# A three-stage transformer kernel: the last recurrent tile by token halves, and reordered starts and ends of four stages

## The chip, the cores and the metric

One core of a Trainium2 chip runs the whole program in one launch. The metric is the device time in microseconds (us). The engines are TensorE (PE), VectorE (DVE), ScalarE (ACT), GpSimd (POOL) and SyncE (SP, which issues all DMAs here). All data is float32.

## What is computed

A sequence of 1024 tokens with 1024 features passes two blocks of two layers each. Cut to what the change touches:

```python
def rglru_layer(x, norm_g, w_in, conv_w, conv_b, w_rg, b_rg, w_ig, b_ig, lam, w_out):
    h = rms_norm(x, norm_g)
    u = h @ w_in                                    # 1024 -> 2 * 1280
    xb, gate = u[..., :D_RNN], u[..., D_RNN:]
    xb = causal_depthwise_conv(xb, conv_w, conv_b)  # 4 taps
    r, i = sigmoid(blocks(xb) @ w_rg + b_rg), sigmoid(blocks(xb) @ w_ig + b_ig)
    log_a = -LRU_C * r * softplus(-lam)
    a, bterm = exp(log_a), sqrt(-expm1(2.0 * log_a)) * (i * xb)
    _, hs = lax.associative_scan(_lin_combine, (a, bterm), axis=1)
    return (hs * silu(gate)) @ w_out                # 1280 -> 1024, then x + ...
```

Then come a latent attention layer (its output projection is called `out_b` below), the final norm of the first block (`final1`), a layer of eight differential attention heads beside a chunked state space scan, a sliding window attention layer (its output projection is `out_sw`), and the last RMS norm (`final2`), whose result is stored.

## The kernel before

**Tiles.** Activations lie with features on partitions: 8 tiles of 128 features x 1024 tokens (`resid`). Each product runs at float32 accuracy as three passes: `w_hi*x_hi`, `w_hi*x_lo`, `w_lo*x_hi` (lines 197 to 199), each a 128x512 matmul. A 128-column weight tile (128x1024, `w_raw`) is loaded by DMA into one of two slots, split by ACT into `w_hi` (line 186) and by DVE into `w_lo` (line 192); one whole tile is 48 matmuls. Of the activations, ACT writes the high part (`operand_hi`) and DVE the low part (`operand_lo`). Every engine has its own program order, written out by hand; semaphores join them.

**Start.** `begin` reads the eight input tiles. For each, ACT writes `operand_hi` (line 319) and the square (line 326), DVE writes `operand_lo` (line 340) and adds the square to a sum (line 348), in turn. PE runs the first weight tile behind them into `acc[0]`, then the second into `acc[1]`; two of its eight slices in, it sums the squares over partitions (line 236), and after the fourth it spreads the norm's diagonal (line 244). ACT copies that to SBUF as `factor`.

**Recurrent layer.** `rglru` loops over b = 0..9, 128 channels each. PE: x tile b+1, the two gates' matmuls of b (line 1045, 3.6 us), gate tile b+1. DVE: `u = acc * factor` (line 1148), three taps, the split of the next weights, gate arithmetic, the scan over 1024 tokens (`tensor_tensor_scan`, line 1201) and `y` (line 1204). For b = 0 the first use of `acc[0]` waits for `factor`.

**Its tail.** The output projection `out_a` (`project_halves`) multiplies ten channel tiles by 16 weight tiles: q = 0..7 for the first 512 tokens, q = 8..15 for the second. It starts in b = 9: operands 0 to 8 are `y` of earlier b read back from HBM into `out_a_raw`; operand 9 is `rnn_y` itself. ACT and DVE split operands 0 to 5 (`Ahead.count`) inside `rglru`, 6 to 9 after it. PE runs q = 0 and 1 side by side for six slices, then the last four slices of each. q = 2 uses the slot of q = 0, and its split stands in both engines' order behind operands 10 and 11 (tokens 512 on), which SP loads after `y` of b = 9 has been stored.

**Head stage.** `out_b` ends with `final(1)`: DVE scales the second token half of `resid` by the first block's norm (line 866, eight instructions), and then all engines meet at a barrier. `differential_attention` starts with v and q tiles done, in `acc[0]` and `acc[1]`. PE's first work is the first half of the k tile (`key_half(0, 0)`) into `acc[0]`, so it waits until ACT has copied v out (line 2187). DVE then takes the low parts of q (line 2240), copies the positional rows into `da_kb` (line 2311) and `da_qb`, and takes the low part of the keys (line 2251); only then come the first scores (line 2018).

**End.** In `out_sw`, the last tile (q = 15) is followed by its residual add, its square, 8 small products with the sum of squares (lines 633 and 636), the newton steps (lines 365 to 369), the spread (line 644), eight scalings of 128x512 (line 844) and eight stores (line 605).

## Time and profile before

| what | value |
|---|---|
| runs of the kernel | 2520.18 us median of 3 (2518.3 to 2521.41) |
| the profiled execution: time / span | 2522.0 us / 2520.2 us |
| PE busy | 2418.8 us, 96% of the span |
| DVE, ACT, POOL busy | 1610.2, 1203.2, 181.8 us |
| mean granted TensorE clock | 0.985 of full speed |

A share of the span is a mean over stages; what counts for a change is where PE stands idle and what it waits for there. The granted clock of a stretch is 1.00 at 2.4 GHz and 0.50 at 1.2 GHz.

### The profile page before, as it was taken

To read this page: it belongs to the slowest core of one execution; us is meant where nothing else is said; L and a number is where in the kernel's file an instruction comes from. 1 tells how busy PE (TensorE), PEld (TensorE's weight loads), DVE (VectorE), ACT (ScalarE), POOL (GpSimd) and SP (SyncE) were. 2 spreads that over 40 slices of the span, in tenths; PEclk is the share of its full clock that TensorE was granted. 3 is DMA by queue.
4 is the path that set the end of the run, shared out by engine and by line. 5 is a ranking of instruction groups with operands and counts; after the bars stand their busy time and mean duration, and the time that the engine had idled before them with its cause. 6 is when DMAs were issued, how large, how long until landed. Compare 5 with 4: busy or idle time off the path is not lost. (4 is left out here: it accounts for less than half of the span.)

```text
span 2520.2 us, 31828 instructions
## 1 busy us (share of the span) xinstructions
PE 2418.8 (96%) x12061; PEld 2003.2 (79%) x12061; DVE 1610.2 (64%) x2946; ACT 1203.2 (48%) x2167; POOL 181.8 (7%) x109
## 2 busy tenths in 40 slices
PE   7999899998999999899999999999999999999998
PEld 5777687887888877688888888888787787888776
DVE  6766656436666657666666666653566665888874
ACT  4555533224544543456555555431554534565542
POOL 0000021000000052000000000000112130000022
PEclk9999999999999999899999999999999999999998
DMA  3222332112221331111101111224543421111133
GB/s 132 80 71 88 127 94 68 61 68 87 79 87 51 113 111 57 42 43 34 43 26 42 34 43 34 83 100 148 192 148 133 142 93 45 34 51 51 51 129 110
DMA packets 91891, 203.22 MB, mean 81 GB/s; under 512 B 10208, under 2 KB 43104, under 8 KB 90720
## 3 DMA queue, kind: packets, MB, share of 16 engines
q1 hardware_dynamic: 91744, 201.25, 23.5%
q8 instruction: 94, 1.54, 0.3%
q14 instruction: 53, 0.43, 0.1%
HBM read 160.26 MB, written 40.96 MB: 80 GB/s over the span
## 5 line engine op out<-in xcount | busy, mean ns | idle before, releaser
L197 PE MATMUL acc<-operand_hi,w_hi 128*128 128x512 f32 x1822 | 739.2, 406 | 42.1 <-DVE w_lo L192 12.7
L199 PE MATMUL acc<-operand_hi,w_lo 128*128 128x512 f32 x1822 | 716.4, 393 | 0.0
L198 PE MATMUL acc<-operand_lo,w_hi 128*128 128x512 f32 x1822 | 715.2, 393 | 0.0
L197 PEld LDWEIGHTS acc<-operand_hi,w_hi 128*128 128x128 f32 x1822 | 345.5, 190 | 120.2 <-issue 19.4
L199 PEld LDWEIGHTS acc<-operand_hi,w_lo 128*128 128x128 f32 x1822 | 344.6, 189 | 75.2
L198 PEld LDWEIGHTS acc<-operand_lo,w_hi 128*128 128x128 f32 x1822 | 345.6, 190 | 68.1 <-issue 3.6
L192 DVE TENSOR_TENSOR w_lo<-w_raw,w_hi 128x1024 fp32r<-128x1024 f32 (+2 forms) x205 | 231.6, 1130 | 173.6 <-ACT w_hi L186 171.8
L186 ACT ACTIVATE w_hi<-w_raw 128x1024 fp32r<-128x1024 f32 (+2 forms) x205 | 199.5, 973 | 275.0 <-PE aux L199 149.0
L197 PE MATMUL aux<-operand_hi,w_hi 128*128 128x512 f32 x634 | 257.4, 406 | 22.5 <-DVE w_lo L192 6.0
L199 PE MATMUL aux<-operand_hi,w_lo 128*128 128x512 f32 x634 | 249.5, 394 | 0.0
L198 PE MATMUL aux<-operand_lo,w_hi 128*128 128x512 f32 x634 | 249.2, 393 | 0.0
L197 PEld LDWEIGHTS aux<-operand_hi,w_hi 128*128 128x128 f32 x634 | 120.5, 190 | 54.5 <-DVE w_lo L192 13.2
L198 PEld LDWEIGHTS aux<-operand_lo,w_hi 128*128 128x128 f32 x634 | 120.7, 190 | 26.2 <-issue 2.4
L199 PEld LDWEIGHTS aux<-operand_hi,w_lo 128*128 128x128 f32 x634 | 120.3, 190 | 26.0
L2267 DVE TENSOR_REDUCE att<-aux 128x1 f32<-128x256 f32 (+7 forms) x128 | 96.3, 752 | 36.4 <-PE aux L2022 36.1
L2215 ACT ACTIVATE da_pth<-acc 128x512 f32<-128x512 f32 (+2 forms) x96 | 43.8, 490 | 128.6 <-PE acc L2036 128.2
L3286 ACT ACTIVATE sw_pth<-aux 128x512 fp32r<-128x512 f32 x64 | 38.3, 599 | 110.9 <-PE aux L3199 110.9
L884 DVE TENSOR_TENSOR resid<-aux,resid 128x512 f32<-128x512 f32 x55 | 37.9, 689 | 78.7 <-PE aux L199 78.5
L2547 DVE SCALAR_TENSOR_TENSOR ssd_work<-ssd_work,vec 128x1024 f32<-128x1024 f32 x36 | 46.3, 1285 | 45.3 <-ACT ssd_work L2526 42.2
L2046 PEld LDWEIGHTS acc<-da_v,da_pth 128*128 128x128 f32 x576 | 71.0, 196 | 3.7 <-ACT da_pth L2215 1.1
L1624 PE MATMUL acc<-mlah_pth,mlah_v 128*128 128x256 f32 (+1 forms) x320 | 70.1, 366 | 2.6 <-ACT mlah_pth L1747 1.6
L2046 PE MATMUL acc<-da_v,da_pth 128*128 128x128 f32 x576 | 71.4, 280 | 0.7 <-ACT da_pth L2215 0.7
(432 smaller groups left out, 4060.3 us busy)
## 6 DMA issues: line engine op xcount, KB each, us to landing
w_raw<-in_stream SPq DMA_DIRECT2D x201, 512.0 KB, 3.7
ssd_e<-cs_scratch SPq DMA_DIRECT2D x8, 1024.0 KB, 6.7
g_scratch<-ssd_work SPq DMA_DIRECT2D x12, 512.0 KB, 2.9
ssd_xbc<-g_scratch SPq DMA_DIRECT2D x8, 768.0 KB, 4.8
y_scratch<-rnn_y SPq DMA_DIRECT2D x10, 512.0 KB, 2.6
out_a_raw<-y_scratch SPq DMA_DIRECT2D x20, 256.0 KB, 4.2
resid<-in_x SPq DMA_DIRECT2D x8, 512.0 KB, 8.5
g_scratch<-mlai_g SPq DMA_DIRECT2D x8, 512.0 KB, 2.9
```

Source lines behind the costliest of these rows:

```text
L186: act.activation(k.w_hi_sb[:, t.slot, 0:width], k.w_raw[:, t.slot, 0:width], ACT.Copy).then_inc(k.w_hi[t.slot], 1)
L192: dve.tensor_tensor(k.w_lo_sb[:, t.slot, 0:width], k.w_raw[:, t.slot, 0:width], as_f32(k.w_hi_sb[:, t.slot, 0:width]), ALU.subtract).then_ ...
L197: pe.matmul(out, w_hi, x_hi, start=first, stop=False)
L198: pe.matmul(out, w_hi, x_lo, start=False, stop=False)
L199: return pe.matmul(out, w_lo, x_hi, start=False, stop=last)
L884: dve.tensor_tensor(resid(q), total(q), resid(q), ALU.add).then_inc(k.acc_free[t.slot], 1)
L1624: mm = pe.matmul(out_v[:, q], v[:, kt * P:(kt + 1) * P], pth[g_ % 2][:, kt, q], start=kt == 0, stop=kt == 2 * g_ + 1)
L2046: mm = pe.matmul(out_v[:, e * P:(e + 1) * P], pth[:, kt, e * P:(e + 1) * P], v[:, kt * P:(kt + 1) * P], start=kt == 0, stop=kt == 2 * g_ + e)
L2215: act.activation(pth[:, at:at + w, (t % 2) * P:(t % 2 + 1) * P], slots[at // 4][:, 0:w * P].rearrange("p (n q) -> p n q", q=P), ACT.Copy). ...
L2267: dve.reduce_max(st[:, 0, :], k.aux[:, m, 0:att_keys(t)], AX.X).then_inc(s["top"], 1)
L2547: link(dve.scalar_tensor_tensor(out=xc[:, :], in0=u[:, tap:tap + S], scalar=k.vec[:, bass.ds(VEC["conv_w2"] + 12 * tap + b, 1)], in1=xc[:, ...
L3286: act.activation(pth[:, n % 2, :], turned, ACT.Copy).then_inc(s["pth"], 1)
```

## The change

Five places, all of the same arithmetic:

1. `begin`: weight tile 0 is loaded first and split first; ACT and DVE split all eight input tiles before any square is taken; the sum of squares is read by PE after six slices of the second tile, the spread comes behind that tile. `acc[0]` is copied raw into `rnn_u`, and the norm's factor is applied there.
2. `rglru`, b = 9: the gates' Tanh move ahead of the silu's Tanh; the last of scaling, scan and `y` run by token halves, with operands 6 to 9 split in between; SP loads operands 10 to 15 in front of the last store of `y`. PE runs eight slices of q = 0 and 1 side by side instead of six.
3. `out_b`: `final(1)` goes. ACT keeps the factor (`kept_factor`), and each of the eight steps of head 0 does one of the eight scalings.
4. `differential_attention`: the first half of head 0's keys goes into the free bank `aux[1]`, second half; three slices of the second half stand before the scores; POOL copies the positional rows; DVE's q work is reordered.
5. `out_sw`: tile 15 runs by quarters of 256 tokens, each with its own sum, factor, scaling and stores.

`begin`: SP, PE and ACT.

```diff
+        sp.dma_start(k.w_raw[:, 0, :], k.stream[0]).then_inc(k.w_loaded[0], 16)
+        sp.dma_start(k.vec[:, :], vec).then_inc(s["vecs"], 16)
         for d in range(DT):
             sp.dma_start(k.resid[:, d, :], x_t[d]).then_inc(s[f"x{d}"], 16)
...
-            if kt == 1:
+            if kt == DT - 1:
+                mm.then_inc(k.tile_done[tiles[1].slot], 1)
+            if kt == 5:
                 pe.wait_ge(s["fill"], 6)
                 pe.wait_ge(s["sum"], DT - 1)
                 stats_pe_sum(pe, k, s, 0, ss, 0)
-            if kt == 3:
-                stats_pe_spread(pe, k, s, 0, rb)
-        mm.then_inc(k.tile_done[tiles[1].slot], 1)
+        stats_pe_spread(pe, k, s, 0, rb)
...
+        act.wait_ge(k.tile_done[tiles[0].slot], 1)
+        act.activation(ahead.u[:, 3:S + 3], k.acc[:, 0, :], ACT.Copy).then_inc(k.acc_free[tiles[0].slot], 1)
         stats_act(act, k, s, 0)
```

`rglru`: SP in front of the last store, and DVE in b = 9 behind its last full-width instruction.

```diff
+                for q in range(RNN_TILES, 16):
+                    ahead.load_y(sp, q)
             sp.wait_ge(s["y"], b + 1)
...
+        ahead.low(dve, 6)
+        dve.wait_ge(s["bi"], last + 1)
+        dve.wait_ge(s["root"], last + 1)
+        scaled_input(0)
+        dve.wait_ge(s["bt0"], 1)
+        dve.tensor_tensor_scan(thr[:, half(0)], a[:, half(0)], bi[:, half(0)], 0.0, ALU.mult, ALU.add
+                               ).then_inc(s["scan0"], 1)
+        ahead.low(dve, 7)
+        dve.wait_ge(s["scan0"], 1)
...
+        gated(0)
+        ahead.low(dve, 8)
+        ahead.low(dve, 9)
+        scaled_input(1)
+        dve.wait_ge(s["bt"], last + 1)
+        dve.tensor_tensor_scan(thr[:, half(1)], a[:, half(1)], bi[:, half(1)], thr[:, HALF - 1:HALF], ALU.mult, ALU.add
+                               ).then_inc(s["scan"], 1)
+        dve.wait_ge(s["scan"], last + 1)
+        gated(1)
```

`project_halves`: PE's lead in `out_a`, and ACT and DVE at the end of `out_b`.

```diff
-            for kt in range(0 if sequential else kts - 4):
+            rest = kts - (2 if done else 4)
+            for kt in range(0 if sequential else rest):
...
         roots(1)
+        if double:
+            act.wait_ge(s["rb"], 2)
+            act.activation(k.kept[:, :], factors(1, 0), ACT.Copy)
...
-        if double:
-            final(1)
```

`differential_attention`: PE, POOL, DVE's first work, and DVE's step t.

```diff
         key_half(0, 0, range(DT))
+        key_half(0, 1, range(3))
         pe.wait_ge(k.acc_free[q_tile(0).slot], q_tile(0).before + 1)
         turn_values(0)
         scores(0, 0)
-        key_half(0, 1, range(DT))
+        key_half(0, 1, range(3, DT))
...
+    @block.gpsimd
+    def _(pool):
+        pool.wait_ge(s["tab_k"], 16)
+        for m in range(2):
+            pool.tensor_copy(kb[64:128, m, :], g[64:128, :]).then_inc(s["kbr"], 1)
...
-        for n in range(2):
-            queries(0, n, k.acc[:, 1, :])
-        dve.wait_ge(s["tab_k"], 16)
-        for m in range(2):
-            dve.tensor_copy(kb[64:128, m, :], g[64:128, :]).then_inc(s["kbr"], 1)
         dve.wait_ge(s["tab_q"], 16)
         first = k.vec[64:128, VEC["slope8"]:VEC["slope8"] + 1]
         dve.tensor_scalar(qb[64:128, 0, :], o[64:128, 0, :], first, None, ALU.mult)
+        queries(0, 0, k.acc[:, 1, :])
         dve.tensor_scalar(qb[64:128, 1, :], o[64:128, 0, :], first, None, ALU.mult).then_inc(s["qbr"], 1)
+        queries(0, 1, k.acc[:, 1, :])
         keys(0, 0)
...
+                if not b:
+                    x = k.resid[:, t, half(1)]
+                    dve.scalar_tensor_tensor(out=x, in0=x, scalar=k.vec[:, VEC["final1"] + t:VEC["final1"] + t + 1],
+                                             in1=k.kept[:, :], op0=ALU.mult, op1=ALU.mult)
```

`project_halves` for `out_sw`: PE in tile 15, and DVE.

```diff
+            for c in range(2):
+                for kt in range(DT):
...
+                    if c and kt == 3:
+                        quarter_squares(0)
+            quarter_spread(0)
+            quarter_squares(1)
+            quarter_spread(1)
...
+            quarter_variance(0)
+            quarter_factor(0)
+            dve.wait_ge(k.tile_done[t.slot], t.before + 1)
+            dve.tensor_tensor(quarter(resid(final_q), 1), last_total[1], quarter(resid(final_q), 1), ALU.add
+                              ).then_inc(k.acc_free[t.slot], 1)
+            dve.wait_ge(s["rb"], 2)
+            for d in range(3):
+                quarter_scaled(0, d)
+            quarter_variance(1)
+            quarter_scaled(0, 3)
+            quarter_factor(1)
+            for d in range(4, DT):
+                quarter_scaled(0, d)
+            dve.wait_ge(s["rb"], 3)
+            for d in range(DT):
+                quarter_scaled(1, d)
```

How the instructions move at two places. First DVE in b = 9 of the recurrent layer, before (`rnn_thi` holds the scan's input, `out_a_lo` with `rnn_y` is operand 9, the last `w_lo` is q = 2's):

```order
L1189 SCALAR_TENSOR_TENSOR rnn_t<-rnn_a,rnn_t 128x1024
L1196 SCALAR_TENSOR_TENSOR rnn_thi<-rnn_thi,rnn_a 128x1024
L1201 SCALAR_TENSOR_TENSOR rnn_y<-rnn_a,rnn_thi 128x1024
L1204 SCALAR_TENSOR_TENSOR rnn_y<-rnn_y,rnn_sg 128x1024
L562 TENSOR_TENSOR operand_lo<-out_a_raw,operand_hi 128x512 x2
L562 TENSOR_TENSOR out_a_lo<-out_a_raw,out_a_hi 128x512
L562 TENSOR_TENSOR out_a_lo<-rnn_y,out_a_hi 128x512
L562 TENSOR_TENSOR operand_lo<-out_a_raw,operand_hi 128x512 x2
L192 TENSOR_TENSOR w_lo<-w_raw,w_hi 128x1024
```

and in the changed kernel:

```order
L573 TENSOR_TENSOR operand_lo<-out_a_raw,operand_hi 128x512
L1339 SCALAR_TENSOR_TENSOR rnn_thi<-rnn_thi,rnn_a 128x512
L1352 SCALAR_TENSOR_TENSOR rnn_thr<-rnn_a,rnn_thi 128x512
L573 TENSOR_TENSOR operand_lo<-out_a_raw,operand_hi 128x512
L1344 SCALAR_TENSOR_TENSOR rnn_y<-rnn_thr,rnn_sg 128x512
L573 TENSOR_TENSOR out_a_lo<-out_a_raw,out_a_hi 128x512
L573 TENSOR_TENSOR out_a_lo<-rnn_y,out_a_hi 128x512
L1339 SCALAR_TENSOR_TENSOR rnn_thi<-rnn_thi,rnn_a 128x512
L1363 SCALAR_TENSOR_TENSOR rnn_thr<-rnn_a,rnn_thr,rnn_thi 128x512
L1344 SCALAR_TENSOR_TENSOR rnn_y<-rnn_thr,rnn_sg 128x512
L573 TENSOR_TENSOR operand_lo<-out_a_raw,operand_hi 128x512 x2
L192 TENSOR_TENSOR w_lo<-w_raw,w_hi 128x1024
```

Operands 6, 7 and 8 no longer stand behind the whole scan, operand 9 needs only its first half, and the second half stands before q = 2's weights. Second, PE at the start of the heads, before (the first line is the last pass of the first half of the keys):

```order
L199 MATMUL acc<-operand_hi,w_lo 128x512
L1997 MATMUL acc<-ident,da_vt 128x128 x8
L2018 MATMUL aux<-da_ka,da_qa 128x128
L2020 MATMUL aux<-mask_r,ident_r 128x128
L2022 MATMUL aux<-da_kb,da_qb 128x128
```

and in the changed kernel:

```order
L199 MATMUL aux<-operand_hi,w_lo 128x512
L197 MATMUL acc<-operand_hi,w_hi 128x512
L198 MATMUL acc<-operand_lo,w_hi 128x512
L199 MATMUL acc<-operand_hi,w_lo 128x512
L2157 MATMUL acc<-ident,da_vt 128x128 x8
L2180 MATMUL aux<-da_ka,da_qa 128x128
L2182 MATMUL aux<-mask_r,ident_r 128x128
L2184 MATMUL aux<-da_kb,da_qb 128x128
```

The first half of the keys is now written to `aux`, and three slices (nine matmuls, of which three are shown) of the second half come ahead of the turning of v.

## Rows read from the trace of the kernel before

**Rows 1.** The page: PE's busy time, its share, its instructions.
```profile
PE 2418.8 (96%) x12061; PEld 2003.2 (79%) x12061; DVE 1610.2 (64%) x2946; ACT 1203.2 (48%) x2167; POOL 181.8 (7%) x109
```
**Rows 2.** Waits of PE over the span: total us, times, longest us.
```profile
PE acc L197 <- ACT da_vt L2187: 8.1, 1, 8.1
...
PE aux L197 <- DVE out_a_w2l L538: 4.2, 1, 4.2
...
PE aux L2018 <- DVE da_kb L2251: 2.5, 1, 2.5
```
**Rows 3.** Timeline, start and early recurrent layer: start us, us, instruction [idle before].
```profile
9.86 0.80 PE L197 MATMUL acc<-operand_hi,w_hi 128*128 128x512 f32 x1 [9.86 <-DVE w_lo L192]
...
23.56 0.50 PE L197 MATMUL acc<-operand_hi,w_hi 128*128 128x512 f32 x1 [0.67 <-DVE operand_lo L340]
...
28.17 0.50 PE L197 MATMUL acc<-operand_hi,w_hi 128*128 128x512 f32 x1 [0.62 <-DVE w_lo L192]
...
31.07 1.84 PE L236 MATMUL aux<-inv_col,stat_sq 128*128 128x1 f32 x16
...
54.17 1.22 DVE L192 TENSOR_TENSOR w_lo<-w_raw,w_hi 128x1024 fp32r<-128x1024 f32 x1
...
54.42 3.60 PE L1045 MATMUL aux<-rnn_xc,rnn_r 128*128 128x512 f32 x8
...
80.45 1.22 DVE L192 TENSOR_TENSOR w_lo<-w_raw,w_hi 128x1024 fp32r<-128x1024 f32 x1
```
**Rows 4.** Waits of DVE from 75 to 262 us, the recurrent layer.
```profile
DVE rnn_u L1148 <- PE acc L199: 28.9, 7, 4.4
```
**Rows 5.** Timeline of the recurrent layer's tail.
```profile
285.67 2.29 DVE L1201 TENSOR_TENSOR_SCAN rnn_y<-rnn_a,rnn_thi 128x1024 f32<-128x1024 f32 x1
...
289.88 0.79 PE L197 MATMUL acc<-operand_hi,w_hi 128*128 128x512 f32 x1 [4.97 <-DVE operand_lo L562]
...
299.70 1.23 DVE L192 TENSOR_TENSOR w_lo<-w_raw,w_hi 128x1024 fp32r<-128x1024 f32 x1 [0.33 <-ACT w_hi L186]
```
**Rows 6.** Windows: stretch, length, PE, PEld, DVE, ACT, POOL busy, clock, DMA share, GB/s.
```profile
301.40:306.90 5.50, 5.50 (x13) 4.34 (x14) 4.29 (x5) 3.55 (x6) 2.41 (x2) 0.50 0.36 119
...
1027.40:1033.90 6.50, 6.50 (x18) 5.35 (x19) 3.15 (x10) 3.35 (x8) 0.00 (x0) 0.50 0.26 83
...
2505.10:2512.20 7.10, 4.59 (x15) 2.93 (x14) 1.94 (x11) 0.20 (x1) 0.00 (x0) 0.50 0.00 0
```
**Rows 7.** Timeline of the start of the heads.
```profile
1008.79 5.35 DVE L866 SCALAR_TENSOR_TENSOR resid<-resid,vec,aux 128x512 f32<-128x512 f32 x8
...
1015.42 1.02 ACT L2187 ACTIVATE da_vt<-acc 128x1024 f32<-128x1024 f32 x1 [7.80 <-PEq L85]
...
1021.47 1.29 DVE L2311 CAST da_kb<-da_g 64x1024 fp32r<-64x1024 f32 x2
...
1026.53 0.69 DVE L2251 TENSOR_TENSOR da_kb<-acc,da_ka 64x512 fp32r<-64x512 f32 x1 [0.54 <-ACT da_ka L2137]
```
**Rows 8.** DMA issues from 1015 to 1020 us: KB, us to landing.
```profile
da_o<-in_tables SPq DMA_DIRECT2D x1, 256.0 KB, 4.1
```
**Rows 9.** POOL's groups by form: busy us, mean ns.
```profile
L782 POOL MEMSET stat_sq<- 128x1024 f32 x4 | 3.8, 958 | 811.9 <-PE acc L1624 411.5 <-DMA y_scratch<-stat_sq 347.5 <-PE aux L244 37.8
L1335 POOL TENSOR_TENSOR stat_sq<-stat_sq,mlai_sq 128x1024 f32<-128x1024 f32 x1 | 2.8, 2757 | 35.2 <-ACT mlai_sq L1372 35.2
```
**Rows 10.** Timeline of PE: 256-column passes, and the end.
```profile
2136.93 0.28 PE L197 MATMUL aux<-sw_pth,sw_v_hi 128*128 128x256 f32 x1
2137.05 0.28 PE L198 MATMUL aux<-sw_ptl,sw_v_hi 128*128 128x256 f32 x1
...
2502.35 0.39 PE L198 MATMUL aux<-operand_lo,w_hi 128*128 128x512 f32 x1
...
2502.58 0.39 PE L199 MATMUL aux<-operand_hi,w_lo 128*128 128x512 f32 x1
```
**Rows 11.** Timeline of DVE: the last scalings.
```profile
2512.14 5.36 DVE L844 SCALAR_TENSOR_TENSOR resid<-resid,vec,aux 128x512 f32<-128x512 f32 x8 [2.17 <-PE aux L644]
```

More of the change, by code:

```diff
@@ L448, in project_halves @@
     own = own or {}
+    end = after == "end"
+    final_q = tiles - 1
     if "raw" in own:
@@ L1165, in _ @@
                 dve.wait_ge(s["y"], b)
+            if b == last:
+                split_lo(dve, k, g_tile(b + 1))
+                for q in range(2):
+                    ahead.low(dve, q)
             dve.tensor_tensor(sg[:, :], k.acc[:, g.slot, :], factor[:, :], ALU.mult
@@ L3477, in build @@
         if stop > 2:
[L3478 removed]
+            heads_and_ssd(k, tables, kept)
         k.end_layer()
```

234 lines of the change are left out of this document (166 added, 68 removed).

## The prediction

> **What bounds the kernel.** I read PE's busy share first: 96% [rows 1], so the bound is PE, and only some 100 us of the span can be won without fewer matmuls. Then PE's waits [rows 2]: the reader should look for single long ones, since the change adds no matmul and takes none away. Three lie where the change works: 8.1 and 2.5 us at the start of the heads, 4.2 us in the recurrent tail. A long wait is followed by a stretch at half clock: 0.50 for 5.5 and 6.5 us [rows 6]. Last come the places themselves in order of time [rows 3, 5, 7, 10, 11], each read for what PE waits for there, and what would be late next. A pass of 512 columns takes 0.23 us at full clock [rows 10], so a slice of two banks (six passes) takes 1.37, a tile 10.9.
>
> **1. Start.** PE's first tile starts at 9.86, the second at 28.17 [rows 3]. Seven times it stands about 0.67 us for DVE [rows 3], which makes an `operand_lo` and a sum in turn, and each restart costs some 0.15 more; without them the tile takes 18.3 - 4.7 - 1.0 = 12.6. With the sums moved behind, DVE needs 1.2 to 1.3 per slice, less than PE. ACT's first split starts no later, since weights and table load come ahead of it. First matmul at 9.9, second tile at 22.5: 5.6 us ahead. But nothing behind it starts earlier by that much. Seven sums chained at 1.26 from about 22.0 end at 30.8, and PE reaches its sixth slice at 30.7; the squares' sum stood at 31.07 [rows 3]. So `factor` comes 0.2 us earlier, and all of DVE's work on b = 0 hangs on it. PE's first gates would be done at 52.6 instead of 54.42 + 3.60 = 58.0, and the gate tile's weights are low-split at 54.17 + 1.22 = 55.4 [rows 3]: 2.8 of the lead are gone. One b later PE arrives at 55.4 + 10.9 + 10.9 + 3.6 = 80.8, and the weights are ready at 80.45 + 1.22 = 81.7, where before PE came at 54.42 + 3.60 + 21.8 + 3.6 = 83.4. From then on DVE has slack, 4.4 us per b [rows 4], and the lead holds. **Gain 1.7 + 0.2 = 1.9, I take 1.8.**
>
> **2. Recurrent tail** (times of before). The root ends at 285.67 - 1.3 = 284.4 [rows 5] in both kernels: ACT's gates come earlier, but the root hangs on a chain that the silu's Tanh joins. Before, scaling 1.2, scan 2.3 and `y` 1.2 in full [rows 5], then operands 6 to 9; PE stood 4.97 us [rows 5], then ran 24 passes, the first at a slower pace, to 301.4 - 4.2 = 297.2 [rows 2, 6]. Now DVE does low 6 (0.6, done 285.6), half scaling 0.7, half scan 1.2, low 7 (288.0), half `y` 0.7, low 8, low 9 (290.0). PE takes slices 6 and 7 of both tiles at 285.6 and 288.0, then 12 passes: done at 292.1. The next tile needs DVE's second half (0.7 + 1.2 + 0.7), two lows 1.2, `w_lo` 1.2 and its piece 0.4: 290.0 + 5.4 = 295.4. Before, `w_lo` started at 299.70 [rows 5], because its ACT split stood behind operands loaded after the last store, and PE resumed at 301.4. **Gain 6.0.** PE still stands 3.3 us, so I keep the half clock of 5.5 us behind it [rows 6]; it costs 2.75, which is the bonus if it goes. SP now waits for seven lows in front of the store of `y`; that store comes at 292.6, nobody reads it before operand 19, and q = 4's weights behind it land before q = 2 ends.
>
> **3. Start of the heads.** PE ended at 1016.6 - 8.1 = 1008.5 [rows 2], DVE's eight scalings at 1014.1, and ACT began the stage at 1015.42 [rows 7], 1.3 after DVE. Without them DVE's last work ends at 1008.9, so the stage starts at 1010.2, and PE at once, having a bank of its own: 6.3 us sooner than at 1016.6. ACT's copy of the factor, 0.6, lies in its wait for the first scaling. Then the chain: tables land 4.1 us after issue [rows 8], at 1013.9; DVE's qb row 0.75, q half 1.4, row 0.75, q half 1.4: 1018.1; second key low part 0.7 + 0.7: scores at 1019.5. PE meanwhile does 24 + 9 passes (7.5) and 1.0 of turning, and stands about 0.5. Before, the scores stood at 1026.53 + 0.69 + 0.15 = 1027.4 [rows 7], then came the short passes (1.5) and 24 long ones: 11.7 at 0.43 up to 1033.9, where the half clock ends [rows 6], and 12.3 at 0.23, to 1036.7. Now 6 short passes 0.9 and 15 long 3.4: 1023.8. Difference 12.9. I subtract 0.5 for a chance that the 1.7 us of idle in front lowers the clock. **Gain 12.4.** The eight multiplies, 0.67 each [rows 7], come behind the next maximum, where DVE waits for ACT's exponential; I cost them nothing. If that cover were gone they cost 5.4. POOL's two copies of 64x1024 have no row: a memset of 128x1024 takes 0.96, an add of it 2.76 [rows 9]. One input lies between; I take 1.5, so 1014.4 + 3.1 = 1017.5, hidden; at 2.76 they end at 1020, costing 0.5.
>
> DVE's own two copies of 64x1024 took 1.29 together [rows 7], a subtraction of 128x1024 takes 1.22 [rows 3]: copies run twice as fast. The Trainium skill ("SBUF — State Buffer", the shared port pair) says such fast copies and `tensor_scalar` take a port pair that GpSimd also needs, exclusively, and that the later one blocks entirely. No row of this trace has both together. By that rule DVE's second qb row would stand behind a POOL copy, the q half with it, and the gain here would be about 1.5 less; this is a rival below, priced by the 1.5 of a copy.
>
> **4. End.** A 256-column pass takes 0.12 [rows 10]: 48 take 5.7 against 24 at 0.23 = 5.5. With 0.9 for the four small products that now stand inside, PE ends at 2504.2 instead of 2503.0. Behind it: DVE's add 0.45, square 0.4, half as many small products (0.9 to 1.7), variance and root 0.5, newton 1.0, diagonal 0.45, spread 0.5 to 1.0, what is left of quarter 0's scalings 0.8, eight scalings of 256 at 0.40 = 3.2 against 8 at 0.67 = 5.36 [rows 11], store 2.7 as before. Sum 11.3 to 12.6, plus DVE's and SP's queues 0.7: end at 2516.2 to 2517.5. Stores are 24 instead of 16, issued at 0.45 each, just slower than the scalings; that is in the 0.7. The half clock behind 2505 [rows 6] stays. **Gain 3.3, I take 3.1.**
>
> **Sum:** 1.8 + 6.0 + 12.4 + 3.1 = 23.3. The profiled execution took 2522.0 (span 2520.2), 1.8 above the median of the runs; the forecast goes by the median: 2520.2 - 23.3 = **2496.9 us**, 0.9% less. A measurement here tells about 0.2%, 5 us, from no change.
>
> **Rivals.**
> - *Full clock kept* (0.19). If PE's shorter waits no longer lower the clock in the tail, 2.75 more, and 0.5 at the heads: 2493.6. For it: seven gaps of 0.6 to 0.7 at the start leave the clock at full. Against: 3.3 us is nearer to the 4.2 that lowered it.
> - *The head stage gives some back* (0.17). POOL's copy holds up DVE's qb row (1.5), and the idle of 1.7 in front costs a half clock of 6.8 us, as the gap before [rows 6] did (3.4 less the 0.5 counted): 2496.9 + 4.4 = 2501.3.
> - *Multiplies on the path* (0.05). Head 0's DVE chain carries them in full: 2496.9 + 5.4 = 2502.3.
> - *The start's lead lives* (0.05). If DVE's b = 0 work came earlier than its old times, 3.8 more: 2493.1.
> - *Slower* (0.01). POOL's copies have no row of their kind. The first scores now wait for both; above 2.5 us each (1014.4 + 2 x 2.5 = 1019.5) every further us costs two. At (23.3 + 5)/2 + 2.5 = 16.7 us each the kernel is slower by over 0.2%; at 18 each, 2496.9 + 31 = 2528. Against: both bounds of rows 9 are far below.
> - *The change doesn't do what it says* (0.02): barrier, scores' wait and tail stay as they were, only start and end gain, 1.8 + 3.1: 2515.3.
>
> Forecast as summed: 0.51. **Range** 2490 to 2505: full clock with a lead of 3.8 below (2489.8), both give-backs together above (2496.9 + 4.4 + 5.4 = 2506.7, less likely, cut to 2505). Faster 0.97 (all but the last two rivals), same 0.02 (2515.3 is within 5 us of before), slower 0.01.
>
> **What would show it.** Right: second tile of PE at 22 to 23; a wait of PE for `w_lo` of 2 to 3 us near 52 and 1 near 81; slices 6 and 7 with waits of 1 to 2 us; PE's wait in the tail 3 to 3.5 instead of 4.2; the first keys within 2 us of PE's last product; one short wait at the scores; a last scaling of 256 columns every 0.40; some 13 us from the last pass of 256 to the end. Wrong: a wait of PE in head 0 for `da_both`; POOL copies above 2.5; first gates that start the next weights at once (then the start wins more); a half clock that appears at a new place.

## The result, and the profile after

| | before | after |
|---|---|---|
| median, runs beside each other on one chip | 2520.80 us of 4 (2518.30 to 2521.98) | 2499.28 us of 4 (2498.40 to 2504.53) |
| ratio | | 0.9927, 95% interval 0.9914 to 0.9940 |
| the profiled execution: time / span | 2522.0 / 2520.2 us | 2504.5 / 2502.7 us |
| mean granted clock | 0.985 | 0.989 |

By the medians the change takes 21.5 us (0.85%) in this comparison; the ratio in the table, 0.9927, puts it at 0.73%, some 18 us. 23.3 was forecast, 2496.9 against 2499.3 measured, inside the range of 2490 to 2505. A second comparison, with more runs, gave less: 14.3 us (`again`, below). The profiles tell where both numbers come from.

The page of the changed kernel, PE's busy time (before in [rows 1]):

```profile
PE 2414.9 (96%) x12087; PEld 2002.7 (80%) x12087; DVE 1612.8 (64%) x2962; ACT 1205.7 (48%) x2172; POOL 184.1 (7%) x111
```

PE's waits over the span (total us, times, longest us), against [rows 2]:

```profile
PE acc L197 <- DVE w_lo L192: 5.3, 3, 2.9
...
PE aux L197 <- DVE out_a_w2l L548: 2.6, 1, 2.6
...
PE acc L2157 <- DVE da_qa L2409: 1.8, 1, 1.8
```

The wait of 8.1 us for `da_vt` is no longer in the list, the one in the tail fell from 4.2 to 2.6, the one in front of the scores from 2.5 to 0.4 with 1.8 for `da_qa` a little earlier. New is a wait of 2.9 us for `w_lo`, at the start. Now the four places, in the timeline of the changed kernel (start us, us, instruction [idle before]).

**Start**, against [rows 3]:

```profile
10.36 0.77 PE L197 MATMUL acc<-operand_hi,w_hi 128*128 128x512 f32 x1 [10.36 <-DVE operand_lo L343]
...
14.07 3.71 ACT L321 ACTIVATE operand_hi<-resid,vec 128x1024 fp32r<-128x1024 f32 x3 [1.41 <-DMA resid<-in_x]
...
23.88 0.39 PE L197 MATMUL acc<-operand_hi,w_hi 128*128 128x512 f32 x1
...
32.05 1.84 PE L236 MATMUL aux<-inv_col,stat_sq 128*128 128x1 f32 x16
...
39.23 1.03 ACT L333 ACTIVATE begin_factor<-aux 128x1024 f32<-128x1024 f32 x1 [3.87 <-PE aux L244]
...
55.15 1.22 DVE L192 TENSOR_TENSOR w_lo<-w_raw,w_hi 128x1024 fp32r<-128x1024 f32 x1
...
56.42 0.50 PE L197 MATMUL acc<-operand_hi,w_hi 128*128 128x512 f32 x1 [2.87 <-DVE w_lo L192]
```

The stops in PE's first tile are gone: five of 0.67 us for `operand_lo` and one of 0.62 in front of the second tile, six in all. The second tile starts at 23.88 instead of 28.17, 4.3 us ahead. Then PE stands 2.87 us for the low part of the next gate weights, and that comes at 55.15 + 1.22 = 56.4, where before it came at 54.17 + 1.22 = 55.4 [rows 3]: DVE's work on b = 0 is 1.0 us later, not 0.2 earlier. Why: the squares' sum runs at 32.05 instead of 31.07. PE ran without a gap from 10.36 to there, so what counts is when it began, 0.5 later, and how long it ran at half pace: its passes come 0.43 apart up to 15.6, before up to 13.4. ACT's wait of 1.41 us for the fifth input tile cost PE nothing here. Behind the new wait of 2.87 us stands half clock, and with it the lead is gone one b later. In the changed kernel:

```profile
56.80:60.20 3.40, 3.40 (x10) 2.66 (x9) 2.06 (x3) 2.19 (x2) 0.00 (x0) 0.50 0.49 154
...
79.92 3.60 PE L1152 MATMUL aux<-rnn_xc,rnn_r 128*128 128x512 f32 x8
...
81.44 1.22 DVE L192 TENSOR_TENSOR w_lo<-w_raw,w_hi 128x1024 fp32r<-128x1024 f32 x1
```

and before:

```profile
79.66 3.60 PE L1045 MATMUL aux<-rnn_xc,rnn_r 128*128 128x512 f32 x8
```

The gates of b = 1 end at 83.5 instead of 83.3. The next weights are ready at 82.66, so PE no longer waits there.

**Recurrent tail**, against [rows 5]:

```profile
278.42 7.54 SPq L584 DMA_DIRECT2D out_a_raw<-y_scratch  x6
...
286.25 1.23 DVE L1352 TENSOR_TENSOR_SCAN rnn_thr<-rnn_a,rnn_thi 128x512 f32<-128x512 f32 x1
...
290.69 1.28 DVE L1363 TENSOR_TENSOR_SCAN rnn_thr<-rnn_a,rnn_thr,rnn_thi 128x512 f32<-128x512 f32 x1
...
293.83 1.22 DVE L192 TENSOR_TENSOR w_lo<-w_raw,w_hi 128x1024 fp32r<-128x1024 f32 x1
...
295.53 0.59 PE L197 MATMUL aux<-operand_hi,w_hi 128*128 128x512 f32 x1 [2.62 <-DVE out_a_w2l L548]
```

The scan of 1024 tokens (2.29 us) is now two of 1.23 and 1.28; slices 6 and 7 are fed between them and PE has no wait there. That is in part the clock: a half clock of 3.4 us from 278.7 on, which the first profile of before does not have, brings PE to slice 6 later. In the five later profiles without it and with the halves (`constants_split`, `loads_behind`, `two_queues`, `quarters_undone`, `combined`) PE waits 0.8 us there. The weights of q = 2 are split at 293.83 instead of 299.70, and PE starts q = 2 at 295.53 instead of 301.40.

**Start of the heads**, against [rows 7, 8]:

```profile
1005.89 0.47 PE L197 MATMUL aux<-operand_hi,w_hi 128*128 128x512 f32 x1 [1.70 <-PEq L85]
...
1010.17 0.75 DVE L2479 TENSOR_SCALAR da_qb<-da_o,vec 64x1024 fp32r<-64x1024 f32 x1 [5.60 <-DMA da_o<-in_tables]
...
1011.36 2.03 POOL L2274 CAST da_kb<-da_g 64x1024 fp32r<-64x1024 f32 x2 [38.59 <-DMA da_g<-in_tables]
...
1012.34 1.60 DVE L2481 TENSOR_SCALAR da_qb<-da_o,vec 64x1024 fp32r<-64x1024 f32 x1
...
1015.42 1.09 PE L2157 MATMUL acc<-ident,da_vt 128*128 128x128 f32 x8 [1.80 <-DVE da_qa L2409]
...
1016.93 0.30 PE L2180 MATMUL aux<-da_ka,da_qa 128*128 128x128 f32 x1 [0.42 <-DVE da_kb L2421]
```

PE stands 1.70 us between the stages instead of 8.09. The two copies into `da_qb` are the same instruction on the same input, yet the first took 0.75 us and the second, while POOL copied into `da_kb`, took 1.60.

**End**, against [rows 11]:

```profile
2492.10 8.75 SPq L620 DMA_DIRECT2D out_x<-resid  x16
...
2494.61 4.78 DVE L943 SCALAR_TENSOR_TENSOR resid<-resid,vec,aux 128x256 f32<-128x256 f32 x12
...
2494.75 1.22 PE L669 MATMUL aux<-stat_diag,ones 128*128 128x256 f32 x2 [2.07 <-DVE stat_diag L957]
```

DVE scales 256 columns in 0.40 us and is through at 2499.39. SP issues its sixteen stores at 0.55 each, the last until 2500.85, and the span ends at 2502.7.

### The same programs, profiled again

The 31 further runs of the kernel before that stand beside the experiments have a median of 2516.0 (2512.2 to 2523.3), 4.8 us below the first median, though the program is the same; three more on another chip took 2511.3, 2518.7 and 2519.6. So a table by stretches follows, and it holds the experiments' profiles too. A stretch ends where PE stops ahead of a wait that all kernels have: behind the gates' matmuls of b = 9 (274.61 in the changed kernel), at the barrier behind `out_a` (419.90), at the barrier before the heads (1004.19), for the last `da_both` of the heads (1549.08), for the last `w_lo` (2415.42), and at the span's end. The third and the fifth stretch hold nothing of the change.

| profile | to b = 9 | tail | unchanged | heads | unchanged | end | span | clock |
|---|---|---|---|---|---|---|---|---|
| before | 274.35 | 152.39 | 581.76 | 555.48 | 865.13 | 91.09 | 2520.2 | 0.985 |
| before_again | 274.13 | 152.08 | 581.73 | 555.60 | 864.10 | 90.16 | 2517.8 | 0.987 |
| before_third | 274.44 | 150.77 | 581.81 | 551.90 | 860.31 | 90.27 | 2509.5 | 0.991 |
| after | 274.61 | 145.29 | 584.29 | 544.89 | 866.34 | 87.28 | 2502.7 | 0.989 |
| again | 274.69 | 145.27 | 581.69 | 547.09 | 863.80 | 87.36 | 2499.9 | 0.989 |
| start_undone | 274.29 | 143.67 | 582.12 | 545.35 | 863.30 | 87.27 | 2496.0 | 0.993 |
| constants_split | 271.89 | 145.32 | 582.35 | 544.90 | 863.93 | 87.31 | 2495.7 | 0.992 |
| loads_behind | 273.77 | 152.85 | 581.87 | 545.17 | 863.21 | 87.43 | 2504.3 | 0.991 |
| halves_undone | 274.06 | 145.54 | 584.62 | 544.57 | 863.85 | 87.36 | 2500.0 | 0.990 |
| final1_back | 273.80 | 145.14 | 581.59 | 549.68 | 866.02 | 87.37 | 2503.6 | 0.988 |
| qb_first | 273.73 | 145.28 | 581.82 | 544.01 | 865.36 | 87.30 | 2497.5 | 0.990 |
| two_queues | 274.80 | 145.30 | 583.25 | 546.79 | 865.80 | 86.66 | 2502.6 | 0.988 |
| quarters_undone | 274.80 | 145.30 | 582.49 | 544.79 | 864.30 | 91.02 | 2502.7 | 0.989 |
| combined | 273.93 | 145.31 | 582.98 | 543.62 | 865.50 | 86.66 | 2498.0 | 0.990 |

A stretch that an edit does not touch repeats within 0.3 us in many profiles and jumps by 1.6 to 3.6 in others. The next section shows what jumps.

### The profile page after: what moved, and what is told of

Same layout as the page of the kernel before. It is cut to its first block and busy times, and to the rows that moved or that the text cites. A ratio compares the mean times of both kernels' runs of the same rounds, so it can differ in the third digit from the quotient of the medians.

```text
span 2502.7 us, 31909 instructions
## 1 busy us (share of the span) xinstructions
PE 2414.9 (96%) x12087; PEld 2002.7 (80%) x12087; DVE 1612.8 (64%) x2962; ACT 1205.7 (48%) x2172; POOL 184.1 (7%) x111
## 5 line engine op out<-in xcount | busy, mean ns | idle before, releaser
L197 PE MATMUL acc<-operand_hi,w_hi 128*128 128x512 f32 (+1 forms) x1830 | 738.5, 404 | 30.0 <-DVE operand_lo L343 10.4
L199 PE MATMUL acc<-operand_hi,w_lo 128*128 128x512 f32 (+1 forms) x1830 | 717.9, 392 | 0.0
L198 PE MATMUL acc<-operand_lo,w_hi 128*128 128x512 f32 (+1 forms) x1830 | 715.8, 391 | 0.0
```

What stands on the lines that cost most here:

```text
L197: pe.matmul(out, w_hi, x_hi, start=first, stop=False)
L198: pe.matmul(out, w_hi, x_lo, start=False, stop=False)
L199: return pe.matmul(out, w_lo, x_hi, start=False, stop=last)
```

## The experiments

### The spread: `again`, `before_again`, `before_third`

No edit. For `again`:

> The changed kernel once more, for the spread of its landmarks and as the measure of the runs beside it. Its first profile had a span of 2502.7 us, with gates of b = 9 at 271.0, the start of q = 2 in the recurrent tail at 295.5, scores(0, 0) at 1016.9, and half clock at 879 and 295. If half clock periods are placed by chance from run to run, this profile has others and a span from 2497 to 2503; if they belong to the program, the same places come again and the span lies within 0.5 of 2502.7.

For `before_again` and `before_third`:

> The kernel before, profiled again, since its 31 runs beside the experiments lie from 2512.2 to 2523.3 with medians of 2515.6 to 2516.0, 4.5 us below the 2520.2 of the first chip. Theory H (the spread is where half clock falls: the first profile, at a mean clock of 0.985, drew more of it than most): a run at a clock of 0.989 has a span near 2512.5, fewer stretches of half clock, and the missing 7 to 8 us of the first profile's 2520.2 in a few stretches; the one behind the barrier of the heads (1013.5 and 1027.1, 6.8 each) and the one at 300.1 are the candidates. Then part of the gain read from the first profile in those stretches was the draw's. Rival C (another chip, everything a little faster): the same half clock places, and every stretch shorter by the same 0.2%.

> The same kernel a third time, for the spread between its profiles. Theory H: the stretches of PE's landmarks that differ between the three profiles are those in which half clock differs, by 1.7 us for each 3.4 us of it. Rival C: they differ evenly.

**Measured.** `again`: 2501.35 us median of 5 (2497.74 to 2504.52) against 2515.63 of 10; ratio 0.9941, interval 0.9927 to 0.9954. `before_again` 2519.55 and `before_third` 2511.32, one run each on the same chip. The stretch of the first scores in three profiles of one program, and in the changed kernel (windows; the third number from the end of a line is the granted clock, ahead of DMA share and GB/s), first before:

```profile
1027.00:1034.00 7.00, 6.63 (x19) 5.50 (x20) 3.37 (x11) 3.75 (x8) 0.00 (x0) 0.51 0.24 77
```

`before_again`, which adds the window behind the last long wait:

```profile
1027.00:1034.00 7.00, 7.00 (x21) 5.75 (x22) 3.15 (x10) 3.21 (x8) 0.00 (x0) 0.54 0.25 77
2392.00:2399.00 7.00, 4.79 (x26) 3.74 (x26) 6.68 (x22) 3.51 (x11) 0.00 (x0) 1.00 0.27 88
```

`before_third`:

```profile
1027.00:1034.00 7.00, 7.00 (x36) 5.88 (x35) 2.58 (x10) 3.98 (x9) 0.00 (x0) 1.00 0.25 75
```

and in the changed kernel, behind its own first scores and in the half clock that it kept late in the program:

```profile
1017.00:1024.00 7.00, 7.00 (x38) 5.97 (x39) 3.79 (x12) 4.92 (x11) 0.00 (x0) 1.00 0.23 75
2381.30:2388.10 6.80, 6.29 (x23) 5.45 (x23) 5.45 (x20) 3.44 (x13) 0.00 (x0) 0.50 0.19 65
```

PE ran 19 to 21 matmuls in seven busy microseconds of two profiles and 36 in the same window of the third. That is 3.6 us in the heads' stretch (555.5 against 551.9). In the fifth stretch `before_third` had no half clock at all, the first profile 20.4 us of it in four places, and they differ by 4.8 us. Theory H holds in kind: the spread sits in a few stretches. One chip gave both 2517.8 and 2509.5, and the third stretch is the same in all three to 0.1, so the rival of a faster chip does not explain the spread. The price that theory H names, 1.7 us for each 3.4 of half clock, holds in the heads (3.6 for 6.8) and not in the fifth stretch (4.8 for 20.4). Half clock costs less where PE is not what bounds: in the window 2392 to 2399 above PE is busy for 4.79 of 7 us and DVE for 6.68. My expectation of 2497 to 2503 for `again` holds at 2499.9. Yet most places came again: eight of the eleven in the changed kernel's first profile stand in `again` within 0.1 us, the one at 295.7 among them. The one at 879 did not come, and one at 896 did. Of the two candidates named for before, only the one behind the first scores varied in its amount. The tail had 10.2 us of half clock in all three profiles, in the third at other places, and its stretch is 1.6 shorter there.

**What follows.** A gain read from a single pair of profiles contains what half clock each of the two happened to get, here called its draw. By the means of the table (stretches whose code an experiment changed left out) the change gives 274.31 - 274.28 = 0.0 to b = 9, 151.75 - 145.10 = 6.7 in the tail, 554.33 - 545.44 = 8.9 in the heads, 90.51 - 87.34 = 3.2 at the end, and the two unchanged stretches are 0.9 and 1.5 longer, in part by half clock (at 877 to 882 in three profiles, and 16 us on the mean in the fifth stretch against 11 before; the rest was not traced). The sum is 16.4. That agrees with the medians of all runs but the first chip's before, 2516.0 - 2499.9 (nine runs of the changed kernel) = 16.1. Of the first chip's 21.5, some 5 are its runs of before, four out of four above 2518 where eight of the other 31 are. Whether that is chance or the chip was not tried.

### The start: `start_undone` and `constants_split`

`start_undone` puts back the old order of loads, splits and sums, and the direct product:

```diff
-            if kt == 5:
+            if kt == 1:
                 pe.wait_ge(s["fill"], 6)
                 pe.wait_ge(s["sum"], DT - 1)
                 stats_pe_sum(pe, k, s, 0, ss, 0)
...
-                dve.tensor_tensor(u[:, 3:S + 3], u[:, 3:S + 3], factor[:, :], ALU.mult).then_inc(s["u0"], 1)
+            dve.tensor_tensor(u[:, 3:S + 3], k.acc[:, x.slot, :], factor[:, :], ALU.mult
+                              ).then_inc(k.acc_free[x.slot], 1)
```

> The changed kernel with the old start: loads, splits and squares in the old order, sum of squares after two slices, acc[0] multiplied by the factor directly. Landmark: the gates' matmuls of b = 9, at 271.0 in the changed kernel and 270.8 before. Theory A (DVE's work on b = 0 hangs on the factor, and the factor came 1.0 later in the changed kernel, not 0.2 earlier, which ate the lead): within 1 us of 271.0, and the total is unchanged. Theory B (the prediction's 1.8): 272.8. Theory C (the lead of PE's first two tiles lives): 275 or later.

`constants_split`, DVE in `rglru`:

```diff
+        constants_front()
         dve.wait_ge(ahead.factor_ready, 1)
         front(0)
-        constants()
...
                 split_lo(dve, k, g_tile(b + 1))
+                if b == 0:
+                    constants_back()
                 front(b + 1)
```

> The changed kernel, with DVE's constants of the recurrent layer (softplus, casts of ident and mask) taken out from between front(0) and the silu of b = 0: the part that needs nothing goes ahead of the wait for the factor, the part that needs ACT's logarithm behind the low split of the next gate weights. Theory A (DVE's chain of b = 0 behind the factor sets when PE starts gate tile 1; PE stood 2.87 us for it from 53.56): the low split done some 2 us earlier than 56.4, PE's wait under 1 us, the gates of b = 9 at about 269. Rival (ACT's side of b = 0, or a later wait for weights, sets it): the gates of b = 9 stay within 0.5 of 271.0.

**Measured.** `start_undone` 2499.76 us (4 runs, ratio 0.9941, 0.9926 to 0.9956), beside `again` at 0.9941. From its timeline:

```profile
31.00 1.84 PE L236 MATMUL aux<-inv_col,stat_sq 128*128 128x1 f32 x16
...
38.18 1.03 ACT L331 ACTIVATE begin_factor<-aux 128x1024 f32<-128x1024 f32 x1 [3.87 <-PE aux L244]
...
270.69 3.60 PE L1151 MATMUL aux<-rnn_xc,rnn_r 128*128 128x512 f32 x8
```

The gates of b = 9 run at 270.69 with the old start and at 271.01 with the new: theory A, nothing of PE's 4.3 us of lead reaches b = 9. The factor is 1.05 us earlier in the old order (38.18 against 39.23). That distance is a draw in part: in the ten profiles with the new order `factor` starts between 38.34 and 39.40, in the four with the old between 38.02 and 38.34. Even where it came at 38.34 (`qb_first`), the first stretch is only 0.6 shorter than before.

`constants_split` 2498.78 us (4 runs, ratio 0.9937, 0.9921 to 0.9952); its profile:

```profile
49.46 1.22 DVE L192 TENSOR_TENSOR w_lo<-w_raw,w_hi 128x1024 fp32r<-128x1024 f32 x1
...
80.55 0.50 PE L197 MATMUL acc<-operand_hi,w_hi 128*128 128x512 f32 x1 [2.57 <-DVE w_lo L192]
...
268.29 3.60 PE L1152 MATMUL aux<-rnn_xc,rnn_r 128*128 128x512 f32 x8
```

The low split is done at 50.7 instead of 56.4, and PE's wait near 54 is gone. A wait of the same kind and cause takes its place one b later, 2.57 us at 80.5. The gates of b = 9 come at 268.29, 2.7 us earlier; in `combined`, which has the same edit and two short half clocks in this stretch (33.2 and 81.0) where this profile has none, at 270.33, so 0.7. DVE's chain behind the factor sets the start; moving it forward helps by 0.7 to 2.7 against the first profile of the changed kernel, 0.4 to 2.4 against the mean of its stretch, which the median cannot yet tell from nothing.

### The tail: `loads_behind` and `halves_undone`

```diff
                 for q in (2, 3):
                     ahead.load_weights(sp, q)
-                for q in range(RNN_TILES, 16):
-                    ahead.load_y(sp, q)
             sp.wait_ge(s["y"], b + 1)
             sp.dma_start(k.y_dram[b], y[:, :]).then_inc(s["stored"], 16)
         sp.wait_ge(s["triu"], 16)
         sp.wait_ge(s["stored"], 16 * RNN_TILES)
+        for q in range(RNN_TILES, 16):
+            ahead.load_y(sp, q)
```

> The changed kernel with the loads of operands 10 to 15 put back behind the last store of y. Theory L (the tail's gain is the loads': before, the ACT split of q = 2 stood behind operands loaded late, and PE resumed at 301.4): q = 2 starts at 300 to 301.5 instead of 295.5, total +5 to 6 us. Rival H (the halves on DVE carry it, the loads only ride along): q = 2 within 1 us of 295.5, total unchanged.

`halves_undone`, DVE in b = 9 (the helpers `scaled_input` and `gated` and their calls go, the loop's full-width body stays for b = 9):

```diff
-            if b == last:
-                break
             dve.wait_ge(s["bi"], b + 1)
...
-        gated(1)
+        for q in range(ahead.count, RNN_TILES):
+            ahead.low(dve, q)
```

> The changed kernel with b = 9 of the recurrent layer at full width again: scaling, scan and y over 1024 tokens, then the low parts of operands 6 to 9; the loads stay in front. Theory L (the loads carry the tail's gain): DVE then ends y at about 288.2 and the four lows at 290.6, q = 2's low split ends within 0.5 us of where it did with halves, and q = 2 starts at 295.5 to 297, total +0 to 1.5 us. Rival H (the halves carry it): PE stands 4 to 5 us before slice 6, q = 2 at 300 to 301.5, total +5 us.

**Measured.** `loads_behind` 2506.09 us (5 runs, ratio 0.9961, 0.9948 to 0.9974), 4.7 above `again` on the same chip. Its tail, with the halves in place:

```profile
294.58 2.99 SPq L584 DMA_DIRECT2D out_a_raw<-y_scratch  x6
...
302.05 0.77 PE L197 MATMUL aux<-operand_hi,w_hi 128*128 128x512 f32 x1 [10.37 <-DVE out_a_w2l L548]
```

The loads wait for the store of `y`, the operands for the loads, the split of q = 2's weights stands behind both, and PE waits 10.37 us in one piece. The tail's stretch is 152.85, as before the change. `halves_undone` 2501.78 us (5 runs, ratio 0.9941, 0.9923 to 0.9959):

```profile
285.19 2.29 DVE L1327 TENSOR_TENSOR_SCAN rnn_y<-rnn_a,rnn_thi 128x1024 f32<-128x1024 f32 x1
...
289.40 0.50 PE L197 MATMUL acc<-operand_hi,w_hi 128*128 128x512 f32 x1 [2.49 <-DVE operand_lo L573]
...
296.77 0.47 PE L197 MATMUL aux<-operand_hi,w_hi 128*128 128x512 f32 x1 [1.63 <-DVE out_a_w2l L548]
```

PE stands 2.49 us at slice 6 again, yet q = 2 starts only 1.8 us later, counted from the stretch's beginning (296.77 - 274.06 = 22.7 against 295.53 - 274.61 = 20.9), and behind its wait of 1.63 the clock stays full, where the 2.62 of the changed kernel is followed by 3.4 us at half. The stretch is 145.54 against 145.29. Theory L: the loads carry the tail, 7.6 us of stretch, and the halves, the change's most visible part, give 0.25 us here. Their worth hangs on the draw: `start_undone`, which has the halves and also no half clock behind the wait, has a stretch of 143.67, 1.9 less than `halves_undone`. So the halves are worth 0.3 to 1.9, and the runs don't say whether the shorter wait of 1.63 is what kept the clock full. The new order of the Tanh and PE's longer lead (eight slices instead of six) stayed in both kernels and were not tried alone.

### The heads: `final1_back` and `qb_first`

`final1_back`, DVE at the end of `out_b` and in head 0:

```diff
+        if double:
+            for d in range(DT):
+                x = k.resid[:, d, half(1)]
+                dve.scalar_tensor_tensor(out=x, in0=x, scalar=k.vec[:, VEC["final1"] + d:VEC["final1"] + d + 1],
+                                         in1=factors(1, 0), op0=ALU.mult, op1=ALU.mult)
...
-                if not b:
-                    x = k.resid[:, t, half(1)]
```

> The changed kernel with the eight scalings of the first block's norm back at the end of out_b, none in head 0. My term (they stood on the path ahead of the stage, 5.35 us): PE's first key matmul 5.2 us later, and since head 0 loses its eight multiplies, of which only the last costs PE 0.7, the total is +4.5 to 5. Rival 1 (PE waits for the tables, 4.1 us after the stage's start, whatever DVE does before): also +5, with the wait at the scores unchanged. Rival 2 (the multiplies cost head 0 their full 5.9 us of DVE): total within 1 us of the changed kernel. Rival 3 (the longer gap adds a half clock of 3.4 to 6.8 us behind it): total +6.5 to 8.5.

`qb_first`:

```diff
         dve.tensor_scalar(qb[64:128, 0, :], o[64:128, 0, :], first, None, ALU.mult)
-        queries(0, 0, k.acc[:, 1, :])
         dve.tensor_scalar(qb[64:128, 1, :], o[64:128, 0, :], first, None, ALU.mult).then_inc(s["qbr"], 1)
+        queries(0, 0, k.acc[:, 1, :])
```

> The changed kernel with both copies into da_qb ahead of DVE's first q half, so that the second copy no longer runs while POOL copies into da_kb at 1011.4 to 1013.4, or runs beside its beginning only. Theory P (the second copy took 1.60 instead of 0.75 because POOL held a shared port): the copies take 0.75 each if both end before POOL's begin, and one of them is stretched only by what it overlaps; scores(0, 0) up to 0.9 us earlier. Rival (the second copy is slow for its own sake, its operands or its place): it takes 1.6 again.

**Measured.** `final1_back` 2504.91 us (6 runs, ratio 0.9958, 0.9945 to 0.9971). The start of its heads:

```profile
1000.82 5.35 DVE L1015 SCALAR_TENSOR_TENSOR resid<-resid,vec,aux 128x512 f32<-128x512 f32 x8
...
1007.48 0.77 PE L197 MATMUL aux<-operand_hi,w_hi 128*128 128x512 f32 x1 [6.95 <-PEq L85]
```

PE's wait is 6.95 instead of 1.70, 5.25 more for 5.35 us of DVE. The stretch is 4.8 longer, as expected for my term: the later start costs 5.25, the half clock from 1004.4 to 1011.2 slows PE's first matmuls, but PE waits that much less for `da_qa` (the scores stand 5.4 later after the stage before, 1018.64 - 1000.53 against 1016.93 - 1004.19), and head 0 wins 0.65 by not having the multiplies. Seven of the eight cost nothing in head 0. Against the mean of the stretch, 545.44, `final1_back` is 4.2 longer, so the scalings account for about half of the heads' gain of 8.9. The rest (the free bank, the three slices ahead of the scores, POOL's copies, DVE's order) is read from the timelines; these parts were not undone one by one.

`qb_first`, one run, 2499.3 us:

```profile
1007.53 0.75 DVE L2480 TENSOR_SCALAR da_qb<-da_o,vec 64x1024 fp32r<-64x1024 f32 x1
...
1008.04 2.14 POOL L2274 CAST da_kb<-da_g 64x1024 fp32r<-64x1024 f32 x2 [37.02 <-DMA da_g<-in_tables]
...
1008.32 2.80 DVE L2409 TENSOR_TENSOR da_qa<-acc,da_qa 64x512 fp32r<-64x512 f32 x4
...
1011.17 1.09 PE L2157 MATMUL acc<-ident,da_vt 128*128 128x128 f32 x8 [0.90 <-DVE da_qa L2409]
```

The second copy takes 0.75 us, and PE's wait for `da_qa` falls from 1.80 to 0.90: theory P. `combined`, with the same order, repeats it (0.76). This time POOL's copies began during the last 0.24 us of DVE's and took 2.14 us for the pair instead of 2.03. DVE's subtractions from `acc` (`TENSOR_TENSOR`, 0.70 each) run beside POOL's copies at their usual pace, in both kernels.

### The end: `two_queues` and `quarters_undone`

```diff
-                for d in range(DT):
+                for d in range(0, DT, 1 + c):
                     sp.wait_ge(s["scaled"], DT * (c + 1) + d + 1)
...
+            for d in range(1, DT, 2):
+                act.wait_ge(s["scaled"], 2 * DT + d + 1)
+                act.dma_start(quarter(out[d][:, half(1)], 1), quarter(k.resid[:, d, half(1)], 1)
+                              ).then_inc(s["stored"], 16)
```

> The changed kernel with four of the last eight stores (odd d of the second quarter) issued by ACT instead of SP. Theory S (SP's issue of sixteen quarter stores at 0.55 each, ending 1.5 us behind the last scaling, sets the end): from the last scaling to the end 2.2 us instead of 3.3, total -1 to -1.5. Rival D (the DMA's transfer and landing behind the last scaling set it): total unchanged, within the noise.

`quarters_undone` takes the path of the other projections for the last tile:

```diff
-    end = after == "end"
+    end = False
...
+        if after == "end":
+            sum_squares(1)
+            spread(1)
+            return
```

> The changed kernel with the last tile of out_sw at full width again (half a sum, one factor, eight scalings of 512 columns, sixteen stores). From the profiles: the last tile's start to the end took 3.8 us less with quarters. So +3.8 if that is theirs, +3.1 by the prediction, 0 if the noise between two profiles made it.

**Measured.** `two_queues` 2501.98 us (4 runs, ratio 0.9945, 0.9924 to 0.9966):

```profile
2492.66 7.26 SPq L620 DMA_DIRECT2D out_x<-resid  x12
...
2495.17 4.78 DVE L947 SCALAR_TENSOR_TENSOR resid<-resid,vec,aux 128x256 f32<-128x256 f32 x12
...
2497.64 2.69 ACTq L830 DMA_DIRECT2D out_x<-resid  x4
```

The last scaling ends at 2499.95, SP's last issue at 2499.92, ACT's at 2500.33, and the span at 2502.6: 2.65 us from the last scaling instead of 3.3. The end stretch is 86.66 in both kernels with this edit, against 87.27 to 87.43 in eight without. Theory S is right in kind, but it gives 0.65, not 1 to 1.5: 0.4 us of issue and 2.3 of transfer and landing stay behind the last scaling.

`quarters_undone` 2503.63 us (4 runs, ratio 0.9945, 0.9926 to 0.9964):

```profile
2494.66 5.36 DVE L907 SCALAR_TENSOR_TENSOR resid<-resid,vec,aux 128x512 f32<-128x512 f32 x8 [2.17 <-PE aux L672]
2495.44 4.94 SPq L617 DMA_DIRECT2D out_x<-resid  x8
```

The end stretch is 91.02, 3.7 above 87.34, so the quarters give 3.7 here; the three profiles of before (91.09, 90.16, 90.27) put it at 2.8 to 3.8.

### Four small moves together: `combined`

`constants_split`, `qb_first` and `two_queues`, and the eighth multiply of head 0 moved:

```diff
-                if not b:
+                if not b and t < QT - 1:
...
                 split_lo(dve, k, g_tile(b + 1))
+                if not b:
+                    x = k.resid[:, QT - 1, half(1)]
+                    dve.scalar_tensor_tensor(out=x, in0=x, scalar=k.vec[:, VEC["final1"] + QT - 1:VEC["final1"] + QT],
+                                             in1=k.kept[:, :], op0=ALU.mult, op1=ALU.mult)
```

> The changed kernel with four small moves together: the constants of the recurrent layer split around b = 0, both copies into da_qb ahead of the first q half, the eighth multiply of head 0 behind the low split of the next gate weights, four of the last stores issued by ACT. If each gives what its place shows, 2 + 0.9 + 0.7 + 1.3 = 4.9 us below the changed kernel, near 2494.5. If each lands in slack further on, no difference. The likeliest: 3 us.

**Measured.** 2496.79 us median of 6 (2495.43 to 2499.79), ratio 0.9918, interval 0.9904 to 0.9932. Beside `again` (0.9941, 0.9927 to 0.9954) that is 0.23% less, and against the median of nine runs of the changed kernel, 2499.9, it is 3.1 us, the size expected. By the table, against the means: 0.4 at the start (274.28 - 273.93), 0.7 at the end, 1.8 in the heads (543.62 against 545.44). PE's wait at the turn to head 1, in the changed kernel

```profile
1074.11 0.47 PE L197 MATMUL acc<-operand_hi,w_hi 128*128 128x512 f32 x1 [1.07 <-DVE da_qa L2409]
```

and in `combined`:

```profile
1071.00 0.47 PE L197 MATMUL acc<-operand_hi,w_hi 128*128 128x512 f32 x1 [0.42 <-DVE da_qa L2421]
```

The two intervals overlap at 0.993, so the difference is likely rather than sure; of the kernels run, this is the fastest.

## Why the prediction was right, and where it was not

**Bound and places.** PE was the bound and stayed it (96% before and after), and the time came from the three single long waits and the end, as read. The total was right within 2.4 us in the first comparison, and that closeness is partly luck: 4.8 us of the 21.5 are the first chip's runs of before. With all runs the gain is 16.4, not 23.3. Of the 6.9 too much, 1.8 are the start, 3.5 the heads and 2.4 the unchanged stretches, which came out longer; the tail and the end gave 0.8 more than forecast. The range of 2490 to 2505 holds both medians of the changed kernel.

**1. Start, 1.8 forecast, nothing measured.** The mechanism was right: PE's lead is lost to DVE's chain on b = 0. Two steps failed. The first is "`factor` comes 0.2 us earlier": it came 1.0 later in the first profile, 0.7 on the mean. PE reached its sixth slice at 32.05, not 30.7. It began at 10.36, not 9.9, since ACT's first split of the input started at 7.74, waiting for the tile's DMA, and not at 5.84 as before ("starts no later"); and full clock came at 15.8 instead of 13.35. The second is "the lead holds": the new wait of 2.87 us was foreseen, the half clock behind it was not. It stood there for 3.4 us in all eight profiles that have this wait. Without it PE would have waited one b later until 82.66, 0.6 ahead of before; with it PE came at 83.5. `start_undone` shows the whole part to be worth nothing. The reading of the old start was off too: PE stood five times for `operand_lo` and once for `w_lo`, 4.0 us, not seven times and 4.7; the 12.6 for the tile holds only because each restart costs more than the 0.15 assumed.

**2. Tail, 6.0 forecast, 6.7 measured on the mean.** The start of q = 2 (295.4 forecast, 295.53 measured) came as computed, and PE's wait of 3.3 was 2.62. The waits of 1 to 2 us at slices 6 and 7 did not come: none in this profile, one of 0.8 in others. The half clock behind the wait came in eight of the nine profiles with halves and loads in front, but at 3.4 us instead of the 5.5 I kept, which accounts for the 0.7 more; in `start_undone` it was absent and the stretch 1.6 shorter, the rival of full clock in small. What the working did not say is how the gain divides: it wrote halves and loads into one chain, and the runs give the loads nearly all of it, and the halves 0.3 to 1.9.

**3. Heads, 12.4 forecast, 10.6 in the first pair, 8.9 on the mean.** The part by the barrier held (6.3 forecast, 8.09 - 1.70 = 6.4 measured), and `final1_back` shows 5.25 of it to be the eight scalings. Behind it the scores came 12.7 us after the stage before, not 11.0: 1.7 of the 1.8 missing in the first pair. Four terms were off. The "before" of the subtraction took the half clock up to 1033.9 [rows 6] as the program's, but it was a draw, 3.6 us, absent in `before_third`; that costs the mean 1.2, the first pair nothing. The table landed 4.3 us after its issue, not 4.1 after the stage's start, 0.6 later than I had it. And POOL's copies held up DVE's second row by 0.85 us, which I had as a rival of 1.5 "priced by the 1.5 of a copy"; the copies took 1.0 each, so even the price was too high. The Trainium skill ("SBUF — State Buffer", Terms, the shared port pair) says that the later of the two engines blocks while the other has the port pair; the 0.75 that became 1.60, and 0.75 again once moved, agree with it. The rule deserved to be in the sum, not beside it. "I cost them nothing" was right for seven multiplies; the eighth stands directly before the queries of head 1 and costs PE 0.65, about what the 0.5 held back for the clock covers in the first pair.

**4. End, 3.1 forecast, 3.2 on the mean and 3.7 against `quarters_undone`.** Right. The terms as listed add up to 10.9 to 12.2, not 11.3 to 12.6; with that sum the gain would have been 3.7. "Issued at 0.45 each, just slower than the scalings" was 0.55 against 0.40, so SP's queue, not DVE, ends the program; `two_queues` wins 0.65 by sharing it.

**Rivals.** Full clock kept, multiplies on the path, and the start's lead did not happen as a whole. Of "the head stage gives some back", the port half came true at 0.85 of 1.5; no half clock followed the gap of 1.70 itself; in `again` and `two_queues` 3.4 us of it came at 1016 to 1017, some 2.3 us behind the waits of 2.47 and 2.13 for `da_qa`, and the stretch is 1.9 to 2.2 longer. In `start_undone`, with a wait of 2.19 there, the clock stayed full.

## What to carry to other kernels

Profile both kernels more than once before reading gains of a few microseconds from them: set landmarks at waits that both have, and see in the unchanged stretches how far the half clock alone moves them. When a tail's weights stand late, look first at what loads stand behind a store in the DMA queue; moving six loads in front of it gave nearly all that splitting a scan in halves seemed to give. A wait that a change adds can bring half clock behind it: count that too. A lead of PE is worth nothing while the next weights hang on a chain of another engine that did not move, so follow that chain before counting the lead.
